# Splitting the second norm of a decoder layer: the first 128 tokens' norm, queries and scores ahead of the other columns

## Chip, cores and metric

The kernel runs on one core of a Trainium2 chip. The metric is device time in microseconds (us) of one launch; lower is better. The core has five engines with queues of their own: TensorE (PE, matmuls), VectorE (DVE), ScalarE (ACT), GpSimd (POOL, which here issues the gathers) and SyncE (SP, which issues the weight loads). They meet at semaphores, and 16 DMA engines move the data.

## Reference

One layer of a decoder over 288 tokens (256 of a prompt, 8 samples of 4), D = 1024: adaLN norm, one input projection, a short convolution and a sparse attention, merged and projected, then a second norm and a retrieval of single-neuron experts (PEER). The change touches the last part:

```python
def _peer(h, w_q, sub_keys, u_tab, v_tab):
    ...
    def block_fn(hb):
        q = (hb @ w_q).reshape(PEER_BLOCK, PEER_HEADS, 2, PEER_QDIM // 2).astype(jnp.float32)
        s = jnp.einsum('thpd,phkd->thpk', q, sub_keys.astype(jnp.float32))
        s1, i1 = lax.top_k(s[:, :, 0], PEER_TOPK)
        s2, i2 = lax.top_k(s[:, :, 1], PEER_TOPK)
        ...
        e = jnp.take_along_axis(cidx, top_pos, axis=-1)
        g = jax.nn.softmax(top_s, axis=-1)
        act = jax.nn.gelu(jnp.einsum('thkd,td->thk', u_tab[e], hb).astype(jnp.float32))
        return jnp.einsum('thk,thkd->td', (g * act).astype(hb.dtype), v_tab[e])
...
    h2 = _modulate(_rmsnorm(x, norm2_w), shift2, scale2)
    y = _peer(h2.reshape(-1, D_MODEL), peer_w_q, peer_sub_keys, peer_u, peer_v).reshape(x.shape)
```

Each token picks 8 heads x 16 experts, and for each expert one row of `peer_u` and one of `peer_v` (1024 floats, 4 KB) is read from memory.

## The kernel before

Everything is float32. Activations of the second half are kept transposed: `xT` and `hT` are 8 blocks of 128 channels by columns of tokens (columns 0 to 255 the prompt, 256 to 287 the samples; `hT` has 96 more columns, copies of the samples, so that the third group of tokens fills 128 rows too).

**The second norm.** PE makes the output projection block by block (L800), DVE adds it to `xT` and writes `hT` = `xT` times the scale (L1591 to L1598), ACT squares (L1208), PE sums the squares with a matrix of ones (L499), ACT takes the root of all 288 columns (`deviation`, L1069, into `rstd`). DVE then inverts `rstd` (L1317), multiplies the samples' columns and shifts them (L1602, L1603), and goes through the 8 channel blocks of `hT` with the 256 prompt columns: times `rstd` (L1605), plus the shift (L1607), one signal of `h_ready` each. L1608 makes the copies of the samples.

**Queries and scores.** PE computes 16 query blocks, `j` = 0 to 15, of 8 matmuls with 288 columns each (L843; the trace shows each float32 matmul as two rows). ACT copies each into `qpT` (L1241). `turn_h2(0)` (L832) turns the first 128 tokens of `hT` into rows for the dot products. `score_unit(n)` (L825) multiplies the queries of unit n with the sub-keys; units 0 and 1 are heads 0 and 1 of the first 128 tokens, from unit 2 on a unit has two heads. ACT copies the scores (L1221) and DVE does `route(n)`: top 16 of both sides, top 16 of their sums, and the experts' numbers into `eidx` (L1617 to L1682), at whose end `routed` goes up by one. `SCORE_AFTER` says after which `j` a unit's scores come.

**The gathers.** A slot is one expert of each of 128 tokens. There are 288 slots, 16 to a head, and each needs an indirect DMA of 128 rows of `peer_u` (L1012, `ask_u`) and one of `peer_v` (L1023, `ask_v`), 512 KB each, issued by POOL in one fixed order: u alone at first, v for slot j from u slot j + 12 or so on, then by turns. In this text u16 is the u gather of slot 16, v8 the v gather of slot 8, and so on. `urows` is a ring of NU = 10 buffers, `vrows` one of NV = 13. u gather i waits for the dot product of slot i - 10 (`u_used`); the first of a unit also waits for `routed` (u0, u16, u32, ...). v4 to v7 lie where the weights of queries `j` = 8 to 11 are, and v8 to v11 where those of `j` = 12 to 15 are, so v4 and v8 wait until PE is done with them. DVE's `dot(i)` (L1726) waits for u gather i and multiplies it with the turned tokens; ACT does the gelu and makes diagonal matrices (L1273), and PE adds up the v rows (L894, L896) once all 16 query blocks are done.

**DVE's order.** After the norm: `route(0)`, `route(1)`, then `dot(0)`, `dot(1)`, ... with steps of the next `route` in between: a `route` is a generator with 16 steps, of which two follow each dot while the unit's first slot is within 26.

## Time and profile before

| what | value |
|---|---|
| median of three runs | 1178.35 us (1177.5 to 1179.29) |
| the profiled execution | 1175.52 us, of which its span is 1173.7 us |
| PE busy | 987.4 us (84%) |
| DVE busy | 718.2 us (61%) |
| POOL busy | 573.8 us (49%) |
| ACT busy | 243.1 us (21%) |
| mean DMA rate over the span | 324 GB/s |
| moved by the queue of indirect DMAs | 312.92 MB of 379.90 MB |

The busy shares are means over stages that have different limits, so none of them alone says what sets the time. The 40 slices of the profile's page, 29.3 us each, show the stages; the chain of waits shows who waits for whom in one of them. Times inside the trace are counted from the start of the span.

### The profile page before, as it was taken

The numbers are of one execution on the slowest core, as the hardware profiler recorded it, in microseconds if no ns is written. First come the engines' busy times: TensorE is split into PE (matmuls) and PEld (weight loads), VectorE is DVE, ScalarE is ACT, GpSimd is POOL, SyncE is SP. The second block draws the span as 40 slices with busy tenths as digits, with TensorE's granted clock in tenths as the row PEclk, the third lists the DMA queues.
The fourth block names the chain that finished last, engine by engine and source line by source line (L and its number), as shares of the span: only waits on it lengthen the run. The fifth ranks groups of instructions, "written<-read, shape, count | busy, mean of one in ns | idle before, by whom it ended". The sixth has DMA issues, their size and how long they took to land.

```text
span 1173.7 us, 10777 instructions
## 1 busy us (share of the span) xinstructions
PE 987.4 (84%) x3369; PEld 497.0 (42%) x3369; DVE 718.2 (61%) x1750; ACT 243.1 (21%) x588; POOL 573.8 (49%) x618
## 2 busy tenths in 40 slices
PE   6898888998999999998787777777777777778888
PEld 3346766675677675452232222222222222223233
DVE  3248465888453699757657658568467576544442
ACT  2111222214401123333112111112112121121110
POOL 0201001002000166777777777777777777777750
PEclk9899999999999999999999999999999999999999
DMA  9952333778354499999999999999999999999993
GB/s 334 332 179 79 111 111 126 251 239 278 93 180 170 160 396 339 409 409 409 409 409 409 409 409 410 408 410 410 409 409 408 410 409 409 410 409 409 409 409 157
DMA packets 121324, 379.90 MB, mean 324 GB/s; under 512 B 11580, under 2 KB 21048, under 8 KB 121268
## 3 DMA queue, kind: packets, MB, share of 16 engines
q0 software_dynamic: 86208, 312.92, 68.0%
q1 hardware_dynamic: 34886, 66.19, 16.2%
q8 instruction: 28, 0.46, 0.2%
q14 instruction: 28, 0.23, 0.1%
q10 hardware_dynamic: 174, 0.11, 0.0%
HBM read 377.59 MB, written 1.59 MB: 323 GB/s over the span
## 4 chain that ended last, share of the span: by engine, by line
DMA 34%; PE 34%; POOL 13%; DVE 10%; issue 6%; ACT 2%; SPq 0%; DVEq 0%; ACTq 0%; POOLq 0%
DMA big<-peer_v,oT 16%; DMA big<-peer_u,oT 14%; PE twoA L556 7%; POOL big L1023 7%; POOL big L1012 5%; PE twoD L894 4%; PE twoD L896 4%; PE twoD L800 3%; DMA big<-w_ada 2%; DVE big L1726 2%; PE twoA L534 2%; PE twoA L843 2%; PE twoA L483 2%; PE twoA L704 1%; DMA r<-peer_u,oT 1%
## 5 line engine op out<-in xcount | busy, mean ns | idle before, releaser
L1012 POOL DMA_INDIRECT big<-peer_u,oT x232 | 220.0, 948 | 196.5 <-DVEq L1684 116.6
L1023 POOL DMA_INDIRECT big<-peer_v,oT x266 | 250.4, 941 | 87.9 <-issue 67.4
L1726 DVE CUSTOM_DVE_ANT_0 big<-big,twoA 128x1024 f32<-128x1024 f32 x128 | 156.3, 1221 | 138.8 <-DMA big<-peer_u,oT 137.8
L1726 DVE CUSTOM_DVE_ANT_0 big<-big,twoD 128x1024 f32<-128x1024 f32 x104 | 125.5, 1218 | 58.2 <-DMA big<-peer_u,oT 57.2
L894 PE MATMUL twoD<-big 128*128 128x512 f32 x176 | 97.7, 637 | 44.2 <-DMA big<-peer_v,oT 42.4
L556 PE MATMUL twoA<-hT,big 128*128 128x288 f32 x448 | 116.5, 417 | 0.0
L894 PE MATMUL twoD<-big,modT 128*128 128x512 f32 x132 | 73.2, 637 | 31.1 <-DMA big<-peer_v,oT 30.8
L556 PEld LDWEIGHTS twoA<-hT,big 128*128 128x128 f32 x448 | 85.5, 195 | 28.4 <-issue 5.9
L896 PE MATMUL twoD<-big 128*128 128x512 f32 x176 | 89.9, 592 | 0.0
L894 PEld LDWEIGHTS twoD<-big 128*128 128x128 f32 x176 | 27.0, 188 | 110.4 <-DMA big<-peer_v,oT 105.1
L896 PE MATMUL twoD<-big,modT 128*128 128x512 f32 x132 | 67.4, 592 | 0.0
L894 PE MATMUL twoD<-big,rstd 128*128 128x512 f32 x90 | 49.8, 635 | 19.8 <-DMA big<-peer_v,oT 19.4
L894 PE MATMUL twoD<-big,cT 128*128 128x512 f32 x88 | 48.2, 630 | 21.4 <-DMA big<-peer_v,oT 20.8
L1273 ACT ACTIVATE big<-ctab,oT 128x128 f32<-128x128 f32 x96 | 34.1, 393 | 137.5 <-DVE oT L1705 89.9
L1012 POOL DMA_INDIRECT r<-peer_u,oT x56 | 53.4, 954 | 18.4 <-issue 12.5
L1726 DVE CUSTOM_DVE_ANT_0 r<-r,twoA 128x1024 f32<-128x1024 f32 x32 | 39.0, 1220 | 36.6 <-DMA r<-peer_u,oT 36.6
L1273 ACT ACTIVATE modT<-ctab,oT 128x128 f32<-128x128 f32 x72 | 26.3, 394 | 137.0 <-DVE oT L1705 92.6
L894 PEld LDWEIGHTS twoD<-big,modT 128*128 128x128 f32 x132 | 20.1, 188 | 80.2 <-DMA big<-peer_v,oT 75.8
L896 PEld LDWEIGHTS twoD<-big 128*128 128x128 f32 x176 | 33.4, 190 | 42.1 <-issue 42.1
L843 PE MATMUL twoA<-hT,big 128*128 128x288 f32 x192 | 49.0, 410 | 1.8 <-DVE hT L1607 1.8
L896 PE MATMUL twoD<-big,rstd 128*128 128x512 f32 x90 | 46.0, 592 | 0.0
L896 PE MATMUL twoD<-big,cT 128*128 128x512 f32 x88 | 44.9, 592 | 0.0
(339 smaller groups left out, 1415.6 us busy)
## 6 DMA issues: line engine op xcount, KB each, us to landing
big<-w_ada SPq DMA_DIRECT2D x8, 2048.0 KB, 8.0
big<-w_in SPq DMA_DIRECT2D x5, 2048.0 KB, 8.9
big<-w_in SPq DMA_DIRECT2D x9, 1024.0 KB, 7.5
big<-w_ada SPq DMA_DIRECT2D x2, 4096.0 KB, 23.4
big<-peer_w_q SPq DMA_DIRECT2D x3, 2048.0 KB, 8.4
big<-peer_v,oT POOLq DMA_INDIRECT x266, 19.7
big<-w_out SPq DMA_DIRECT2D x2, 2048.0 KB, 11.5
big<-peer_u,oT POOLq DMA_INDIRECT x232, 17.6
```

The costliest lines, as they stand in the source:

```text
L483: mm = pe.matmul(b[32 * q:32 * q + 32, :], cT[:, k, :], w[:, k, :], start=(k < 4), stop=(k >= 4), skip_group_check=True)
L534: mm = pe.matmul(b[:, 0:width], hT[:, k, COLS[t]:COLS[t] + P], w[:, k, :], start=(k == 0), stop=(k == DC - 1))
L556: mm = pe.matmul(b[:, 0:TOK], w[:, k, j * P:(j + 1) * P], hT[:, k, 0:TOK], start=(k == 0), stop=(k == DC - 1))
L704: mm = pe.matmul(b[:, 0:TOK], slot[0][:, k, j * P:(j + 1) * P], aT[:, k, 0:TOK], start=(k == 0), stop=(k == 3))
L800: mm = pe.matmul(b[:, 0:TOK], w[:, k, (j % 4) * P:(j % 4 + 1) * P], mixT[:, k, :], start=(k == 0), stop=(k == DC - 1))
L843: mm = pe.matmul(b[:, 0:TOK], w[:, k, (j % 4) * P:(j % 4 + 1) * P], hT[:, k, 0:TOK], start=(k == 0), stop=(k == DC - 1))
L894: pe.matmul(acc[0][:, :], diag[j % NDG], row[:, 0:512], start=(s == 0), stop=(s == SLOTS[t] - 1), skip_group_check=True)
L896: mm = pe.matmul(acc[1][:, :], diag[j % NDG], row[:, 512:D], start=(s == 0), stop=(s == SLOTS[t] - 1), skip_group_check=True)
L1012: pool.indirect_dma_start(urows[i % NU], None, peer_u, bass.IndirectOffsetOnAxis(ap=eidx[:, t, s:s + 1], axis=0)).then_inc(u_in[i % NU], 16)
L1023: pool.indirect_dma_start(vrows[j % NV], None, peer_v, bass.IndirectOffsetOnAxis(ap=eidx[:, t, s:s + 1], axis=0)).then_inc(v_in[j % NV], 16)
L1273: act.activation(diag[j % NDG], ident, ACT.Copy, scale=dots[:, t, s:s + 1]).then_inc(diag_ready, 1)
L1726: dve.tensor_tensor_reduce(out=urows[i % NU], in0=urows[i % NU], in1=h2tok[t][:, :], scale=1.0, scalar=0.0, op0=ALU.mult, op1=ALU.add, acc ...
```

## The change

Four things change. (1) The norm after the root is done for columns 0 to 127 first: DVE inverts 128 columns of `rstd`, then goes through the 8 channel blocks with the product of block c ahead of the shift of block c - 1. The other columns follow: inversion of 160, 8 products of 160 columns (`h_scaled`), and ACT, no longer DVE, adds the shift to columns 128 to 255 (`shift_rest`, `h_rest`). (2) PE makes query blocks 0 and 1 for the 128 columns, turns the first tokens, and scores unit 0; only then it makes the 160 other columns of blocks 0 and 1 and goes on with `j` = 2. Turning the sub-keys is spread around the sum of squares, and one of the four turns still waits for the root. (3) DVE does `route(0)`, the copies of the samples, and then dots at once; `route(1)` is cut in: no step after dots 0 to 3, three steps after each dot from 4 on. (4) The u ring begins with buffers that no query weights use, so that u0 no longer waits for the first query weights to be free; u6 does.

```diff
+        urows = urows[4:] + urows[:4]
...
-        H2_BEFORE = 2
+        SUB_ORDER = (0, 2, 1, 3)
...
-        SCORE_AFTER = [1, 4, 8, 12]
+        SCORE_AFTER = [4, 8, 12]
...
             square_sum(DC - 2, 1)
+            pe.wait_ge(sub_landed, 16)
+            turn_sub(SUB_ORDER[0])
+            square_sum(DC - 1, 1)
+            turn_sub(SUB_ORDER[1])
+            turn_sub(SUB_ORDER[2])
+            pe.wait_ge(sd_ready, 2)
+            turn_sub(SUB_ORDER[3])
...
+            first = weights(pe, group("peerq"))
+            for j in range(2):
+                b = A.open(pe)
+                for k in range(DC):
+                    pe.wait_ge(h_ready, DC + k + 1)
+                    mm = pe.matmul(b[:, 0:P], first[:, k, j * P:(j + 1) * P], hT[:, k, 0:P], start=(k == 0), stop=(k == DC - 1))
+                A.close(mm)
+            pe.wait_ge(d_free, V.n)
+            turn_h2(0)
+            score_unit(0)
+            pe.wait_ge(h_ready, 2 * DC + 1)
             for j in range(16):
...
+                b, begin = A.open(pe), P if j < 2 else 0
                 for k in range(DC):
                     if j == 0:
-                        pe.wait_ge(h_ready, DC + k + 1)
+                        pe.wait_ge(h_rest, k + 1)
...
@@ gathers, POOL @@
+                if i == 6:
+                    pool.wait_ge(*released[group("peerq")])
...
-            pool.wait_ge(*released[group("peerq")])
+            pool.wait_ge(*released[group("out", 1)])
...
@@ ScalarE @@
+            for j in range(2):
+                copy_query(j, 0, P)
+            for c in range(4):
+                shift_rest(c)
+            copy_scores()
+            for c in range(4, DC):
+                shift_rest(c)
             for j in range(16):
...
+                copy_query(j, P if j < 2 else 0, TOK)
...
@@ VectorE @@
-            inverse(2)
+            dve.wait_ge(sd_ready, 2)
+            L.tell(dve.reciprocal(rstd[:, 0:P], rstd[:, 0:P]))
+            for c in range(DC + 1):
+                if c < DC:
+                    L.tell(tt(hT[:, c, 0:P], hT[:, c, 0:P], rstd[:, 0:P], ALU.mult), wait=False)
+                if c:
+                    L.done_but(1 if c < DC else 0)
+                    L.tell(ts(hT[:, c - 1, 0:P], hT[:, c - 1, 0:P], modT[:, 23 + c, 0:1], None, ALU.add), h_ready, wait=False)
+            L.tell(dve.reciprocal(rstd[:, P:TOK], rstd[:, P:TOK]))
+            for c in range(DC):
+                L.tell(tt(hT[:, c, P:TOK], hT[:, c, P:TOK], rstd[:, P:TOK], ALU.mult), h_scaled, wait=False)
...
-            for n in range(2):
-                for _ in route(n):
-                    pass
-            found, router = 2, route(2)
+            for _ in route(0):
+                pass
+            L.tell(cp(hT[:, :, TOK:3 * P].rearrange("p c (r t) -> p c r t", t=NSM),
+                      hT[:, :, SEQ:TOK].unsqueeze(2).broadcast_to([P, DC, 3, NSM])), h_ready)
+            found, router = 1, route(1)
...
-                for _ in range(2 if near <= 26 else (1 if found > 2 and near < 44 else 0)):
+                for _ in range((0 if i < 4 else 3) if found == 1 else 2 if near <= 26 else (1 if found > 2 and near < 44 else 0)):
```

On PE, this is what stood between the turned sub-keys and query block 3 (the names after the operation are what it writes and what it reads; `x7` is the number of further matmuls of the block):

```order
L843 MATMUL twoA<-hT,big 128x288 [waits h_ready,a_free,w_landed5]
L843 MATMUL twoA<-hT,big 128x288 [waits h_ready] x7
L843 MATMUL twoA<-hT,big 128x288 [waits a_free]
L843 MATMUL twoA<-hT,big 128x288 x7
L832 MATMUL twoD<-ctab,hT 128x128 [waits h_ready,d_free]
L832 MATMUL twoD<-ctab,hT 128x128 x7
L825 MATMUL twoA<-zall,r 128x128 [waits a_free,qp_ready,subT_ready]
```

And the same place after the change:

```order
L810 MATMUL twoA<-ctab,zall 128x128 [waits a_free,sd_ready]
L810 MATMUL twoA<-ctab,zall 128x128 x3
L846 MATMUL twoA<-hT,big 128x128 [waits h_ready,a_free,w_landed5]
L846 MATMUL twoA<-hT,big 128x128 [waits h_ready] x7
L838 MATMUL twoD<-ctab,hT 128x128 [waits h_ready,d_free]
L838 MATMUL twoD<-ctab,hT 128x128 x7
L831 MATMUL twoA<-zall,r 128x128 [waits a_free,qp_ready,subT_ready]
L860 MATMUL twoA<-hT,big 128x160 [waits a_free,h_rest,w_landed5,h_ready]
L860 MATMUL twoA<-hT,big 128x160 [waits h_rest] x7
```

The scores of unit 0 (L831) now stand behind two blocks of 128 columns, and the blocks of 160 columns behind the scores.

On DVE, right behind the end of `route(0)` (L1681, L1682 before), the whole of `route(1)` stood ahead of the first dot:

```order
L1681 CAST oT<-zall 128x16 [waits dve_seq]
L1682 TENSOR_TENSOR zall<-zall,gsm 128x16
L1617 MAX zall<-r 128x8 [waits s_ready]
L1617 MAX zall<-r 128x8
L1621 MAX_INDEX zall<-zall,r 128x8 [waits dve_seq] x2
```

After the change the dots (two rows each, L1768; `u_in4` is the semaphore of a u buffer) stand there, and `route(1)` between them:

```order
L1724 TENSOR_TENSOR zall<-zall,gsm 128x16
L1773 COPY hT<-hT 128x8x96 [waits dve_seq]
L1768 ISA big,oT<-big,twoD 128x1024 [waits u_in0,h2_ready,h_ready]
...
L1768 ISA r,oT<-r,twoD 128x1024 [waits u_in4]
L1768 ISA oT 128x1
L1659 MAX zall<-r 128x8 [waits s_ready]
L1659 MAX zall<-r 128x8
L1663 MAX_INDEX zall<-zall,r 128x8 [waits dve_seq] x2
L1667 MATCH_REPLACE r<-zall,r 128x128 [waits dve_seq] x2
L1768 ISA r,oT<-r,twoD 128x1024 [waits u_in5]
```

The end of `route(1)`, which u16 waits for, moved from ahead of dot 0 to behind dot 9; the first step of `route(2)` follows it directly.

On POOL the first gathers were eight, two and six u gathers, v0 and u16:

```order
L1012 DMA big<-peer_u,oT 128x1024 [waits routed,a_full]
L1012 DMA big<-peer_u,oT 128x1024 x7
L1012 DMA r<-peer_u,oT 128x1024 x2
L1012 DMA big<-peer_u,oT 128x1024 [waits u_used] x6
L1023 DMA big<-peer_v,oT 128x1024
L1012 DMA big<-peer_u,oT 128x1024 [waits u_used,routed]
```

They are now

```order
L1029 DMA big<-peer_u,oT 128x1024 [waits routed,d_full]
L1029 DMA big<-peer_u,oT 128x1024 x3
L1029 DMA r<-peer_u,oT 128x1024 x2
L1029 DMA big<-peer_u,oT 128x1024 [waits a_full]
L1029 DMA big<-peer_u,oT 128x1024 x3
L1029 DMA big<-peer_u,oT 128x1024 [waits u_used] x4
L1029 DMA r<-peer_u,oT 128x1024 [waits u_used] x2
L1040 DMA big<-peer_v,oT 128x1024
L1029 DMA big<-peer_u,oT 128x1024 [waits u_used,routed]
```

The order of slots is the same; the wait for the query weights (`a_full`) moved from u0 to u6.

## Rows read from the trace of the kernel before

**Rows 1.** The page: DMA rate in 40 slices of 29.3 us.

```profile
GB/s 334 332 179 79 111 111 126 251 239 278 93 180 170 160 396 339 409 409 409 409 409 409 409 409 410 408 410 410 409 409 408 410 409 409 410 409 409 409 409 157
```

**Rows 2.** Stretches: length, then busy us of each engine, granted clock, DMA share, GB/s.

```profile
405.00:410.00 5.00, 5.00 (x24) 4.01 (x23) 2.56 (x18) 0.80 (x2) 3.78 (x5) 1.00 0.65 202
410.00:415.00 5.00, 5.00 (x23) 3.90 (x22) 4.79 (x19) 0.75 (x2) 3.78 (x5) 1.00 0.95 313
415.00:440.00 25.00, 25.00 (x113) 19.98 (x112) 24.48 (x84) 6.29 (x13) 17.00 (x18) 1.00 1.02 409
440.00:460.00 20.00, 17.89 (x68) 12.07 (x67) 19.71 (x54) 8.95 (x22) 12.51 (x15) 1.00 0.90 306
480.00:1150.00 670.00, 533.46 (x1180) 194.26 (x1179) 410.94 (x976) 127.59 (x337) 491.88 (x521) 1.00 1.03 409
```

**Rows 3.** POOL in order of time: u0, u1, u16, u24, v8.

```profile
404.73 0.94 POOL L1012 DMA_INDIRECT big<-peer_u,oT  x1 [116.64 <-DVEq L1684]
405.97 0.94 POOL L1012 DMA_INDIRECT big<-peer_u,oT  x1 [0.30 <-issue]
...
426.47 0.94 POOL L1012 DMA_INDIRECT big<-peer_u,oT  x1 [0.30 <-issue]
...
449.10 0.94 POOL L1012 DMA_INDIRECT big<-peer_u,oT  x1 [1.03 <-DVE oT L1726]
...
454.73 0.93 POOL L1023 DMA_INDIRECT big<-peer_v,oT  x1 [0.30 <-issue]
```

**Rows 4.** The tile peer_u, 400 to 470 us: from issue to landing.

```profile
DMA to landing us min/median/max: 4.1/6.6/7.9
```

**Rows 5.** DVE in order of time: the norm, both first routes, dots, route 2.

```profile
380.13 1.95 DVE L1317 RECIPROCAL rstd<-rstd 128x288 f32<-128x288 f32 x1 [1.37 <-ACT rstd L1069]
...
383.37 0.35 DVE L1607 TENSOR_SCALAR hT<-hT,modT 128x256 f32<-128x256 f32 x1
383.64 0.42 DVE L1605 TENSOR_TENSOR hT<-hT,rstd 128x256 f32<-128x256 f32 x1
...
395.31 0.49 DVE L1617 MAX8 zall<-r 128x8 f32<-128x128 f32 x2 [6.07 <-ACT r L1221]
...
407.40 0.49 DVE L1617 MAX8 zall<-r 128x8 f32<-128x128 f32 x2 [3.51 <-ACT r L1221]
...
415.83 0.17 DVE L1682 TENSOR_TENSOR zall<-zall,gsm 128x16 f32<-128x16 f32 x1
416.28 1.22 DVE L1726 CUSTOM_DVE_ANT_0 big<-big,twoD 128x1024 f32<-128x1024 f32 x1 [0.28 <-DVE zall L1682]
...
423.13 1.22 DVE L1726 CUSTOM_DVE_ANT_0 big<-big,twoD 128x1024 f32<-128x1024 f32 x1
...
446.99 0.18 DVE L1682 TENSOR_TENSOR zall<-zall,gsm 128x32 f32<-128x32 f32 x1
```

**Rows 6.** PE in order of time: query blocks, turn, scores.

```profile
383.87 9.59 PE L843 MATMUL twoA<-hT,big 128*128 128x288 f32 x32 [1.75 <-DVE hT L1607]
393.30 1.04 PE L832 MATMUL twoD<-ctab,hT 128*128 128x128 f32 x8
394.17 0.61 PE L825 MATMUL twoA<-zall,r 128*128 128x128 f32 x4
394.62 7.93 PE L843 MATMUL twoA<-hT,big 128*128 128x288 f32 x32
...
439.53 11.81 PE L843 MATMUL twoA<-hT,big 128*128 128x288 f32 x48
```

**Rows 7.** ACT in order of time: copies of query 1, of its scores, gelu 1.

```profile
393.50 0.41 ACT L1241 ACTIVATE r<-twoA 128x288 f32<-128x288 f32 x1 [3.47 <-PE twoA L843]
394.82 0.38 ACT L1221 ACTIVATE r<-twoA 128x256 f32<-128x256 f32 x1 [0.91 <-PE twoA L825]
...
450.53 0.21 ACT L1237 ACTIVATE oT<-oT 128x8 f32<-128x8 f32 x1 [7.29 <-DVE oT L1726]
```

**Rows 8.** A stretch near the start, columns as in group 2.

```profile
40.00:50.00 10.00, 7.34 (x27) 3.68 (x28) 7.21 (x22) 0.80 (x2) 0.77 (x1) 0.66 1.07 373
```

More of the change, by code:

```diff
@@ L804, in _, with turn_sub @@
                     square_sum(j - 2, 1)
-            square_sum(DC - 2, 1)
-            square_sum(DC - 1, 1)
-            pe.wait_ge(sd_ready, 2)
-            pe.wait_ge(sub_landed, 16)
-            for q in range(4):
+            def turn_sub(q):
                 b = A.open(pe)
@@ L838, in _ @@
                     w = weights(pe, g)
-                b = A.open(pe)
+                b, begin = A.open(pe), P if j < 2 else 0
                 for k in range(DC):
                     if j == 0:
-                        pe.wait_ge(h_ready, DC + k + 1)
-                    mm = pe.matmul(b[:, 0:TOK], w[:, k, (j % 4) * P:(j % 4 + 1) * P], hT[:, k, 0:TOK], start=(k == 0), stop=(k == DC - 1))
+                        pe.wait_ge(h_rest, k + 1)
+                    mm = pe.matmul(b[:, begin:TOK], w[:, k, (j % 4) * P:(j % 4 + 1) * P], hT[:, k, begin:TOK], start=(k == 0),
+                                   stop=(k == DC - 1))
                 A.close(mm)
                 released[g] = (a_full, A.n)
-                if j == H2_BEFORE - 1:
-                    pe.wait_ge(d_free, V.n)
-                    turn_h2(0)
                 if j in SCORE_AFTER:
-                    score_unit(SCORE_AFTER.index(j))
+                    score_unit(SCORE_AFTER.index(j) + 1)
             score_unit(4)
@@ L1208, in _, with copy_sub @@
                 L.tell(act.activation(sq[:, c * TOK:(c + 1) * TOK], xT[:, c, :], ACT.Square), sq_ready)
-            deviation(1)
-            act.wait_ge(sub_landed, 16)
-            for q in range(4):
+            def copy_sub(q):
                 b = A.take(act)
@@ L1215, in _ @@
                 act.sem_inc(a_free, 1)
+            act.wait_ge(sub_landed, 16)
+            copy_sub(SUB_ORDER[0])
+            deviation(1)
+            for q in SUB_ORDER[1:]:
+                copy_sub(q)
             def copy_scores():
@@ L1237, in gelus, with copy_query, shift_rest @@
                 L.tell(act.activation(chunk, chunk, ACT.Gelu_apprx_tanh), gelu_done, wait=False)
+            def copy_query(j, a, e):
+                b = A.take(act)
+                L.tell(act.activation(qpT[:, j, a:e], b[:, a:e], ACT.Copy), qp_ready)
+                act.sem_inc(a_free, 1)
+            def shift_rest(c):
+                act.wait_ge(h_scaled, c + 1)
+                L.tell(act.activation(hT[:, c, P:SEQ], hT[:, c, P:SEQ], ACT.Identity, bias=modT[:, 24 + c, 0:1]), h_rest, wait=False)
+            for j in range(2):
[5 more added lines that the diff above has]
+                shift_rest(c)
             for j in range(16):
-                b = A.take(act)
-                L.tell(act.activation(qpT[:, j, :], b[:, 0:TOK], ACT.Copy), qp_ready)
-                act.sem_inc(a_free, 1)
+                copy_query(j, P if j < 2 else 0, TOK)
                 if j in SCORE_AFTER:
@@ L1599, in _ @@
                           ab[:, j, 1:9].unsqueeze(2).broadcast_to([P, NB, NS]), ALU.mult), wait=False)
[L1600 to L1609 removed]
+            dve.wait_ge(sd_ready, 2)
[9 more added lines that the diff above has]
+                L.tell(tt(hT[:, c, P:TOK], hT[:, c, P:TOK], rstd[:, P:TOK], ALU.mult), h_scaled, wait=False)
+            dve.wait_ge(h_scaled, DC)
+            hs = hT[:, :, SEQ:TOK].rearrange("p c (b s) -> p c b s", s=NS)
+            L.tell(tt(hs, hs, modT[:, 24:24 + DC, 1:9].unsqueeze(3).broadcast_to([P, DC, NB, NS]), ALU.add), h_ready)
             def top16(n, values, best, place):
```

15 lines of the change are left out of this document (4 added, 11 removed).

## The prediction

> **What bounds the kernel now.** I read the slices of the page first: from the 17th on the DMA engines move 409 GB/s without a break almost to the end [rows 1]. From 480 to 1150 us the DMA share is 1.03 while PE, DVE and POOL all have idle time [rows 2]. So the long second part is a fixed quantity of bytes at a fixed rate: 576 gathers of 0.524 MB at 409 GB/s, 1.281 us each, 738 us in all. PE's tail behind the last gather stays as it is. What can change is when the gathers begin, and how much DMA time is lost until the queue is full for good.
>
> The stretches give both. u0 is issued at 404.73 [rows 3]. From there to 415 the engines move 2.58 MB in 10.3 us, which at full rate are 6.3: a cold start costs 4.0. Then 409 GB/s up to 440; from 440 to 460 it is 306, a loss of 5.0 [rows 2]. The sum over these stretches is 18.9 MB, 36 gathers, which in POOL's order are u0 to u26 and v0 to v8. **My yardstick: in the kernel before, gather 36 is through at 460.0, and from then on nothing is lost.** If it is through earlier by x in the changed kernel, and nothing is lost later, the kernel is faster by x.
>
> The loss from 440 to 460 is DVE's. POOL waits for a dot ahead of u24 [rows 3], because from 424.3 to 447.2 DVE has only seven dots (7 to 13) beside the 16 steps of `route(2)` [rows 5].
>
> **The change step by step.**
>
> *The start of the gathers.* Today the inversion of 288 columns begins at 380.13 and takes 1.95; a product of 256 columns takes 0.42 and a shift 0.35, with 0.27 between the starts of two that don't wait for each other [rows 5]. Of 128 columns the inversion is about 0.95 (in proportion, and a little fixed): 381.1. With products and shifts interleaved none waits for its predecessor, so a pair is between 0.27 (two instructions at 256 columns' 0.27, halved) and 0.45. I take 0.32: first product 0.3, eight pairs 2.6, last shift ready at 384.2. PE follows with query 0 (ends 384.4). The trace has matmuls of 128 columns in the scores and the turn: the turn's 8 rows take 0.87 from start to start of the next, 0.11 each [rows 6]. Query 1 is 16 such rows, 1.8: 386.2. The turn makes it 387.1, the scores 387.6 and 387.8 to their end. ACT has copied query 1 by 386.7, does four shifts of some 0.25 and is free at 387.8; copying the scores takes 0.38 [rows 7]. DVE begins `route(0)` at 388.4 instead of 395.31 [rows 5]: 6.9 earlier. Nothing between it and u0 changes except that u0 needs no query weights: u0 at 397.8.
>
> *The second route.* Today `route(1)` ends at 416.0 [rows 5], and u16 needs it only at 426.47 [rows 3], so it holds no gather up. Now dots 0 to 4 come first. A u gather takes 4.1 to 7.9 from issue to landing, median 6.6 [rows 4]; by bytes five gathers are through 10.4 after u0's issue [rows 2], and u4's issue at +5.0 with the median is +11.6. I take 11.2: dot 4 runs from 409.0 to 410.2. The 16 steps of `route(1)` have five dots (5 to 9) between them. The route takes 8.6 alone (407.40 to 416.0) and a dot 1.14 [rows 5], together 14.3: `routed` at 424.5, and u16 0.8 later, as u0 after `route(0)`, at **425.3**. POOL, issuing every 1.24 [rows 3], has u0 to u15 and v0 out by 418.9; the engines are through with these 17 at 397.8 + 4.0 + 21.8 = 423.6 and run dry. So the early start turns into a wait, and u16 comes only 1.2 earlier than today.
>
> *After it.* 19 gathers remain to number 36. A second cold start of 4.0 and 19 x 1.281 = 24.3 give 453.6, if POOL isn't held up. DVE then holds nothing up: at 424.5 it has done 10 dots and two routes, today 7 at 424.3. `route(2)` with seven dots takes 22.9 as today, so dot 16 is done at about 445, and u26 wants it at 425.3 + 17 x 1.24 = 446.4. The loss of 5.0 goes.
>
> *PE's queries.* v8 would be issued at 447.6, but its buffer holds query weights until block 15 is done. The 160-column blocks can start behind the scores and the samples' shift at about 387.9; 32 rows of 0.135 (0.243 for 288 columns, in proportion [rows 6]) take 4.3, so block 2 starts at 392.3 instead of 394.6, if ACT's last four shifts (388.2 to 389.2) keep ahead, as they do by a hair. Everything behind is as before, hence block 15 ends at 449.0 instead of 451.3 [rows 6], and v8 goes out at 449.3. Today v8 is issued at 454.73 [rows 3] and is through 5.3 later. The same 5.3 gives **454.6**, later than 453.6. The later one decides: x = 5.4.
>
> *Edits at nothing.* The first turn of sub-keys and its copy lie in PE's wait for the last square; if that cover fails, up to 0.7 on the start. The copies for the samples (0.55) lie between `route(0)` and the landing of u0, the shifts moved to ACT in its idle time ahead of the scores. u6 waits for block 3, which ends at about 400.1 against u6 at 405.2. ACT's gelu 1 waits for dot 15 (today until 450.53 [rows 7]), now at about 441, so PE's banks are freed sooner.
>
> **Rule against trace.** In the trace a shift starts 0.27 after the one ahead when it needn't wait for it [rows 5]: a fixed part is hidden. The Trainium skill, "VectorE: DVE Perf Modes", section on the TRN2 errata, says the reverse of such splits: each instruction on SBUF pays a fixed latency between instructions, so that small tiles pay it more often, and for a float32 product it gives (N + 151) / 0.96 ns. This case's row agrees for 256 columns alone (0.42). As an estimate by that page, a pair of 128 columns would be 0.58 and the start 2.1 later; u16 at 427.4, the 36th gather at 455.7, x = 4.3. By the rows it is 5.4, which I keep. The difference is small because v8's wait swallows it.
>
> **Unknown costs and their bounds.** The pair on DVE: 0.27 to 0.45, the start -0.4 to +1.0. The second cold start: 4.0 when it is as the first; not below 2.9 (4.1 to the first landing less one transfer). Shifts on ACT: if PE waits for each, block 2 is up to 1.5 later, x down to 3.9. Stalls for dots, today 5.0: from none to all. A pause of POOL at v8 on top of a queue filled only since 425: nothing to 1.2. Good ends together give x = 7.1 (v8 at its 447.6), bad ones without the stalls 2.8.
>
> **The rivals.**
> - *A, forecast:* u16 waits for the later `route(1)`, the stalls at 440 to 460 go, v8 waits for PE. 1175.5 - 5.4 = 1170.1 in the profiled execution's own time, 1173.0 as a median (the shown one lies 2.8 above the profiled time). Chance 0.50, own range 1171.2 to 1175.0.
> - *B, more is kept:* `route(1)` ends sooner than I think (landings quicker, steps hidden behind dots), the queue doesn't run dry, and PE finishes some us earlier too. For it speaks the start lead of 6.9, against it block 15, tied to 57 us of PE's work from block 2 on. x = 7 to 9, 1170.3. Chance 0.15.
> - *C, the gain drains away:* DVE is again late with dots behind u16, since the same work lies ahead of slot 32. Part or all of the 5.0 comes back: x = 0.4 to 2.4, 1177.0. For it speaks that DVE has only 1.4 to spare at u26; against it that the DMA backlog covers a pause of POOL. Chance 0.20. Here belongs also that the start comes hardly earlier: u16 is tied to u0 at +27.5, and with u0 after 401 no 2.4 is left.
> - *D, slower:* TensorE's clock. It is granted in full (1.00, the 2.4 GHz level) in this stretch although PE waits for DVE there [rows 2]. From 40 to 50 us, where PE was busy 7.34 of 10 with short groups and gaps, the grant was 0.66, a part of it at the 1.2 GHz level [rows 8]. The new 378 to 389 has such short groups. At the lower level PE loses half its time: 11 us of it shift v8 to 454.8, and the gain is gone; with 16 us v8 goes out at 457.3 and the kernel is 2.6 slower, 1181.0. Chance 0.07.
> - The rest, 0.08, is spread over both sides.
>
> **The numbers.** A measurement of this kernel tells some 0.2% (2.4 us) from no change. Faster by more: A, B, and a little of C and the rest, 0.77; within: most of C, 0.16; slower: D and a bit, 0.07. The range for 8 in 10 goes from B's low end to the middle of C: 1169.5 to 1177.2.
>
> **What would show it.** u0 at 397.8 (wrong beyond 1.0), `route(0)` from 388.4. POOL waiting some 6 us ahead of u16, for DVE, until 425.3; a hole in the DMA rate at about 424 to 429. No wait for a dot at u20 to u26. v8 released by PE at about 449.3, block 2 starting at 392.3. From 460 on 409 GB/s as today, and the last gather 5.4 earlier. It is wrong if u16 comes after 430, if the rate from 440 to 460 is again near 306, or if the granted clock falls below 1.00 between 380 and 450.

## The result, and the profile of the changed kernel

The changed kernel takes 1170.3 us as the median of 8 runs (1169.63 to 1175.08), the kernel before 1177.41 beside it (8 runs, 1176.27 to 1180.62): a ratio of 0.9942, 95% interval 0.9927 to 0.9957, 6.8 us faster (5.1 to 8.6). The two medians stand 7.1 apart. The forecast was 5.4 us and 1173.0. The profiled execution took 1169.63 us, its span 1167.8: 5.9 less than that of before.

The page, DMA rate in 40 slices. The rate is steady from the 17th slice on, as in [rows 1], and at the same height; the three slices ahead of it moved more than before (238, 346 and 380 GB/s against 160, 396 and 339).

```profile
GB/s 332 339 177 79 128 94 127 252 234 283 97 181 148 238 346 380 410 409 409 409 409 410 408 410 409 409 410 410 409 409 409 410 409 409 409 409 410 408 410 162
```

Stretches, columns as in [rows 2]: length, busy us of each engine, granted clock, DMA share, GB/s.

```profile
398.00:405.00 7.00, 7.00 (x33) 5.58 (x32) 1.80 (x3) 1.06 (x3) 5.48 (x6) 1.00 0.72 225
405.00:410.00 5.00, 5.00 (x22) 3.95 (x21) 4.23 (x7) 0.55 (x2) 3.78 (x5) 1.00 0.99 355
410.00:420.00 10.00, 10.00 (x43) 7.79 (x43) 9.79 (x39) 0.82 (x2) 6.61 (x8) 1.00 1.02 411
420.00:435.00 15.00, 15.00 (x68) 11.96 (x67) 14.62 (x61) 5.23 (x9) 8.09 (x9) 1.00 0.81 284
435.00:450.00 15.00, 14.50 (x66) 11.31 (x65) 14.70 (x41) 5.12 (x9) 10.39 (x11) 1.00 1.03 410
450.00:460.00 10.00, 8.70 (x22) 4.08 (x22) 10.00 (x36) 4.62 (x14) 7.56 (x9) 0.83 0.94 324
460.00:480.00 20.00, 20.00 (x46) 7.79 (x45) 13.05 (x41) 5.48 (x12) 15.12 (x17) 1.00 1.03 410
480.00:1150.00 670.00, 536.86 (x1189) 196.38 (x1188) 413.99 (x983) 128.41 (x340) 487.67 (x517) 1.00 1.02 408
```

The forecast hole is there: 284 GB/s from 420 to 435. The stalls of 440 to 460 are gone up to 450 (410 GB/s); from 450 to 460 a smaller hole is left, 324.

POOL in order of time: u0, v0, u16, v7, the u gather behind it, v8; in brackets the idle time ahead and what ended it.

```profile
397.91 0.94 POOL L1029 DMA_INDIRECT big<-peer_u,oT  x1 [110.75 <-DVEq L1726]
...
417.80 0.94 POOL L1040 DMA_INDIRECT big<-peer_v,oT  x1 [0.30 <-issue]
424.47 0.93 POOL L1029 DMA_INDIRECT big<-peer_u,oT  x1 [5.73 <-DVEq L1726]
...
444.88 1.40 POOL L1040 DMA_INDIRECT big<-peer_v,oT  x1 [0.30 <-issue]
446.58 0.94 POOL L1029 DMA_INDIRECT big<-peer_u,oT  x1 [0.31 <-issue]
449.38 0.94 POOL L1040 DMA_INDIRECT big<-peer_v,oT  x1 [1.86 <-PE twoA L860]
```

POOL waits 5.73 us at u16 for the end of `route(1)` (the signal behind L1724, which is L1726), as the forecast said, then for no dot, and 1.86 at v8 for PE's last query block.

DVE in order of time: the norm of 128 columns, that of 160, the first steps of `route(0)`, dots 0 and 4, the end of `route(1)`, and the first step of `route(2)`.

```profile
379.80 0.95 DVE L1639 RECIPROCAL rstd<-rstd 128x128 f32<-128x128 f32 x1 [1.33 <-ACT rstd L1086]
...
382.58 0.28 DVE L1642 TENSOR_TENSOR hT<-hT,rstd 128x128 f32<-128x128 f32 x1
382.79 0.28 DVE L1645 TENSOR_SCALAR hT<-hT,modT 128x128 f32<-128x128 f32 x1
382.98 0.28 DVE L1642 TENSOR_TENSOR hT<-hT,rstd 128x128 f32<-128x128 f32 x1
...
385.15 1.97 DVE L1648 TENSOR_TENSOR hT<-hT,rstd 128x160 f32<-128x160 f32 x8
...
388.50 0.49 DVE L1659 MAX8 zall<-r 128x8 f32<-128x128 f32 x2 [0.92 <-ACT r L1243]
...
402.16 1.22 DVE L1768 CUSTOM_DVE_ANT_0 big<-big,twoD 128x1024 f32<-128x1024 f32 x1 [4.37 <-DMA big<-peer_u,oT]
...
408.89 1.22 DVE L1768 CUSTOM_DVE_ANT_0 r<-r,twoD 128x1024 f32<-128x1024 f32 x1
...
423.97 0.17 DVE L1724 TENSOR_TENSOR zall<-zall,gsm 128x16 f32<-128x16 f32 x1
424.29 0.87 DVE L1659 MAX8 zall<-r 128x8 f32<-128x128 f32 x4
```

PE in order of time: the short blocks, turn, scores of unit 0, then the 160 other columns of blocks 0 and 1 together with blocks 2 and 3 (one row of 64), and the last three blocks.

```profile
381.62 4.79 PE L846 MATMUL twoA<-hT,big 128*128 128x128 f32 x32 [1.10 <-DVE hT L1645]
386.25 1.04 PE L838 MATMUL twoD<-ctab,hT 128*128 128x128 f32 x8
387.12 0.61 PE L831 MATMUL twoA<-zall,r 128*128 128x128 f32 x4
387.63 12.68 PE L860 MATMUL twoA<-hT,big 128*128 128x160 f32 x64
...
437.30 11.81 PE L860 MATMUL twoA<-hT,big 128*128 128x288 f32 x48
```

**A closer yardstick.** The part of the program ahead of the norm is the same in all kernels but for the turning of the sub-keys, but its length differs between profiled executions: DVE's inversion of `rstd` (I call its start the root) begins at 379.6 to 383.1 us. So I count from the root: u0; then the DMA time lost between u0 and 480, which is that stretch less its bytes at 409 GB/s; then the end of the span. For the changed kernel the rows above hold 29.3 MB, 71.7 us at 409 GB/s, and 480 - 397.9 - 71.7 = 10.4. For the kernel before, [rows 2] give 9.0 up to 460. The other rows of the table are worked out in the same way. The granted clock over the span is 0.984 to 0.988 in them; the last column is explained below the table.

| kernel | u0 | lost | sum | end | end less sum | ratio to before | faster than before, all executions at clock 0.987 |
|---|---|---|---|---|---|---|---|
| before | 24.6 | 9.0 | 33.6 | 793.6 | 760.0 | | |
| changed | 18.1 | 10.4 | 28.5 | 788.0 | 759.5 | 0.9942 | 5.3 (with e5) |
| changed, e5 | 18.1 | 9.9 | 28.0 | 787.0 | 759.0 | 0.9945 | |
| e6, five steps | 18.1 | 15.7 | 33.9 | 794.0 | 760.1 | 0.9994 | 0.6 |
| e7, five steps, v ring | 18.1 | 15.4 | 33.5 | 793.2 | 759.7 | 0.9994 | 0.7 |
| e8, old u ring | 20.8 | 8.7 | 29.5 | 788.8 | 759.3 | 0.9952 | 3.9 |
| e9, steps mended | 18.1 | 10.1 | 28.2 | 788.1 | 759.9 | 0.9953 | 5.7 |
| e10, mended, v ring | 18.1 | 7.7 | 25.8 | 785.5 | 759.7 | 0.9932 | 8.0 |
| e11, v ring | 18.1 | 8.9 | 27.0 | 786.2 | 759.2 | 0.9937 | 6.7 |
| e12, `route(1)` first | 18.1 | 13.5 | 31.6 | 791.5 | 759.9 | 0.9978 | 2.8 |

What is left behind the sum is 759.0 to 760.1 us in all ten. So the end is set by when the gathers begin and by the DMA time lost until the queue stays full, and by nothing else that these edits touch. The sum is an account and no forecast: it takes the lost time from the same trace as the end. From before to changed the start gains 6.5 and the losses take 1.4 back, which leaves 5.1; 5.6 arrive at the end of the span, and the 0.5 between them is within the 1.1 by which the rest differs from profile to profile. The ratio says 6.8, with both inside its interval.

**A second measure, from all executions.** The account rests on one profile of each kernel. The times of all executions bear it out once the granted clock is taken out. Within each kernel a lower mean clock over the span goes with a longer time: 0.97 us for each 0.001 (0.90 to 1.04), by a straight line of one slope through 132 executions (the changed kernel's eight of the result and all of the second and third rounds below). The profiles show where that time lies: the root is at 382.5 to 383.1 us in the four executions at 0.984 and 0.985 (e6, e8, e10, e11) and at 379.6 to 381.7 in the six at 0.987 and 0.988, while "end less sum" is alike in both groups. So it lies ahead of the root. The last column of the table compares all executions at one clock, 0.987, with intervals of 0.5 to 0.7 to both sides; "at one clock" means this comparison from here on. The kernel before stands at 1177.0 us at that clock in the second round and at 1176.9 in the third, so kernels of the two rounds can be compared in this way. The column agrees with the differences of "sum" within 0.9 us in every row, and it tells kernels apart that the ratios alone don't.

### The profile page after: what moved, and what is told of

The parts are those of the page before. It is cut to its first block, busy times and chain, and to the rows that moved or that the text cites. A ratio compares the mean times of both kernels' runs of the same rounds, so it can differ in the third digit from the quotient of the medians.

```text
span 1167.8 us, 10869 instructions
## 1 busy us (share of the span) xinstructions
PE 987.6 (85%) x3401; PEld 500.4 (43%) x3401; DVE 717.3 (61%) x1758; ACT 246.0 (21%) x598; POOL 574.3 (49%) x618
## 4 chain that ended last, share of the span: by engine, by line
PE 39%; DMA 37%; POOL 11%; DVE 6%; issue 5%; ACT 2%; SPq 0%; DVEq 0%; ACTq 0%; POOLq 0%
DMA big<-peer_v,oT 20%; DMA big<-peer_u,oT 12%; PE twoA L557 7%; POOL big L1040 5%; PE twoA L860 5%; PE twoD L909 5%; PE twoD L911 5%; POOL big L1029 4%; PE twoD L801 3%; DMA big<-w_ada 2%; PE twoA L535 2%; PE twoA L484 2%; PE twoA L705 1%; PE twoD L789 1%; POOL r L1029 1%
## 5 line engine op out<-in xcount | busy, mean ns | idle before, releaser
L1029 POOL DMA_INDIRECT big<-peer_u,oT x230 | 217.3, 945 | 188.9 <-DVEq L1726 116.5
L1768 DVE CUSTOM_DVE_ANT_0 big<-big,twoA 128x1024 f32<-128x1024 f32 x128 | 156.3, 1221 | 142.0 <-DMA big<-peer_u,oT 141.0
L1768 DVE CUSTOM_DVE_ANT_0 big<-big,twoD 128x1024 f32<-128x1024 f32 x102 | 123.2, 1217 | 51.3 <-DMA big<-peer_u,oT 50.0
L557 PE MATMUL twoA<-hT,big 128*128 128x288 f32 x448 | 116.0, 415 | 0.0
L909 PEld LDWEIGHTS twoD<-big 128*128 128x128 f32 x176 | 27.5, 190 | 108.2 <-DMA big<-peer_v,oT 101.2
L1768 DVE CUSTOM_DVE_ANT_0 r<-r,twoA 128x1024 f32<-128x1024 f32 x32 | 39.1, 1221 | 33.3 <-DMA r<-peer_u,oT 33.3
L860 PE MATMUL twoA<-hT,big 128*128 128x288 f32 (+1 forms) x192 | 44.2, 390 | 0.0
```

Of the source, the lines that this page charges most:

```text
L557: mm = pe.matmul(b[:, 0:TOK], w[:, k, j * P:(j + 1) * P], hT[:, k, 0:TOK], start=(k == 0), stop=(k == DC - 1))
L860: mm = pe.matmul(b[:, begin:TOK], w[:, k, (j % 4) * P:(j % 4 + 1) * P], hT[:, k, begin:TOK], start=(k == 0), stop=(k == DC - 1))
L909: pe.matmul(acc[0][:, :], diag[j % NDG], row[:, 0:512], start=(s == 0), stop=(s == SLOTS[t] - 1), skip_group_check=True)
L1029: pool.indirect_dma_start(urows[i % NU], None, peer_u, bass.IndirectOffsetOnAxis(ap=eidx[:, t, s:s + 1], axis=0)).then_inc(u_in[i % NU], 16)
L1768: dve.tensor_tensor_reduce(out=urows[i % NU], in0=urows[i % NU], in1=h2tok[t][:, :], scale=1.0, scalar=0.0, op0=ALU.mult, op1=ALU.add, acc ...
```

## The experiments

Twelve runs in three rounds; each run is a set of executions with one of them profiled. In the first round (e1 to e4) the chip granted PE a mean clock of 0.904 to 0.911 over the span, the steady rate was 368 GB/s instead of 409, and the kernel before took 1261.64 us. Its runs are compared with each other alone. In the second the kernel before took 1178.56 us, in the third 1177.76.

**e1, the changed kernel again.** No edit.

> The changed kernel once more, as the yardstick for the kernels of this group. By the accounts of gathers (36 of them through 5.4 us earlier) it should be 5.4 to 7 us faster than the kernel before, ratio 0.994 to 0.9955.

1253.44 us, ratio 0.9938 (0.9918 to 0.9958). The gain is there, but the trace isn't that of the first run: u16 is 49.5 behind the root instead of 44.7, though u0 is at 18.1 in both. Two stretches of e1:

```profile
420.00:425.00 5.00, 1.44 (x6) 0.84 (x5) 1.86 (x5) 0.41 (x1) 2.81 (x4) 1.00 1.03 412
425.00:430.00 5.00, 3.60 (x8) 2.47 (x8) 4.03 (x13) 0.82 (x2) 0.00 (x0) 0.66 0.71 283
```

PE is busy 1.44 of 5 us and DVE 1.86 while the DMA engines are full; PE's rows name no semaphore there but "issue", up to 2.38 us at a time. ACT stands still first: it copies a query block every 3.9 us, at 409.23 for the last time, and begins the next copy only at 421.92, while PE runs on until 421. This lengthens `route(1)`. What the three engines waited for isn't shown.

**e2, `route(1)` ahead of the dots**, in the changed kernel.

```diff
+            for _ in route(1):
+                pass
-            found, router = 1, route(1)
+            found, router = 2, route(2)
...
-                for _ in range((0 if i < 4 else 3) if found == 1 else 2 if near <= 26 else (1 if found > 2 and near < 44 else 0)):
+                for _ in range(2 if near <= 26 else (1 if found > 2 and near < 44 else 0)):
```

> The changed kernel with the second route again ahead of the first dot. Theory (the lead is kept because DVE does ten dots before the route of unit 2, which takes the stalls at u20 to u26 away): u0 stays at 397.9; the route starts with its scores at 405 and ends at 413.8, dot 0 at 415, u10 waits for it, u16 goes out at 423.9, half a us earlier than in the changed kernel; but then everything is the kernel before shifted by 2.5 us, with POOL waiting for dots ahead of u18 to u25, v8 at 452.3: 2.5 us faster than before, 3 us slower than the changed kernel. Rival (only the early start counts, the place of the second route is neutral): as fast as the changed kernel, 5 to 7 us faster than before.

1254.23 us, 0.993 (0.9902 to 0.9957): not to be told from e1. The waits for dots were back in its trace, but e1 had the stall just shown, and this round couldn't weigh one against the other.

**e3, the new order alone**: parts 3 and 4 of the change on the kernel before, the norm unsplit.

```diff
+        urows = urows[4:] + urows[:4]
...
+                if i == 6:
+                    pool.wait_ge(*released[group("peerq")])
...
-            pool.wait_ge(*released[group("peerq")])
+            pool.wait_ge(*released[group("out", 1)])
...
-            for n in range(2):
-                for _ in route(n):
-                    pass
-            found, router = 2, route(2)
+            for _ in route(0):
+                pass
+            found, router = 1, route(1)
...
-                for _ in range(2 if near <= 26 else (1 if found > 2 and near < 44 else 0)):
+                for _ in range((0 if i < 4 else 3) if found == 1 else 2 if near <= 26 else (1 if found > 2 and near < 44 else 0)):
```

> The kernel before with the other two parts alone: the second route between the dots and the u ring turned round, but the norm, queries and scores as before. Theory (u16 hangs on u0 by 26.6 us): u0 at 404.7, u16 at 431.3, a hole in the DMA rate of 6 us of POOL's time ahead of it, no stall for dots later, v8 at about 454: no change, -0.3 to +0.2%. Rival (the new order of DVE is worth the 5 us of stalls by itself): 3 to 5 us faster than before.

1264.89 us, 1.0028 (1.0014 to 1.0043): a little slower. The rival is out; the upper end of my theory's range, 0.2% slower, lies inside the interval, but u16 went out at 441.44 and not at 431.3. Its profile has the stall of e1 in a worse form, and behind it a hole. Here PE's row names ACT, whose copy of a block that was done at 423.9 begins at 434.16:

```profile
430.00:435.00 5.00, 0.38 (x2) 0.38 (x2) 2.20 (x7) 0.72 (x2) 0.93 (x1) 0.57 1.03 410
435.00:440.00 5.00, 5.00 (x21) 4.19 (x21) 4.90 (x16) 3.23 (x5) 0.00 (x0) 0.75 0.14 52
...
434.62 2.08 PE L826 MATMUL twoA<-zall,r 128*128 128x128 f32 x8 [6.88 <-ACT r L1244]
```

The order alone wasn't run again in a later round, so whether it is slower at the higher clock stays open. It is shown only that in this round it brought nothing by itself.

**e4, v ring**: the one v buffer on which no query weights lie moved from the 13th place of the ring to the 5th, so that v8 lies where blocks 8 to 11 were, and v9 is the first to wait for block 15.

```diff
-        vrows += [part(D)]
+        vrows.insert(4, part(D))
+        v_wring.insert(4, v_wring.pop())
```

> The changed kernel with the v buffer that does not lie in the last query weights moved from place 12 to place 4 of the ring, so that v9 and not v8 is the first to wait for query block 15. Theory (the pause of 1.9 us ahead of v8 costs the 2.1 us that the DMA engines lose between 450 and 460): POOL does not wait at v8 nor at v9 (due at 450.3, block 15 ends at 449.1), the rate is 409 GB/s from 435 on, 1.5 to 2 us faster than the changed kernel. Rival (the queue is deep enough, the loss at 450 to 460 has another cause): no change against the changed kernel.

1252.94 us, 0.9928 (0.9904 to 0.9952), against 0.9938 of e1: not told apart.

**e5, the changed kernel a third time**, with e6 to e8.

> The changed kernel again as the yardstick of this group: ratio 0.993 to 0.9955 to the kernel before.

1171.94 us against 1178.56, 0.9945 (0.9925 to 0.9966). u0 and v8 stand at the same distance from the root as in the first run, within 0.01, and u16 0.34 later.

**e6, `route(1)` faster**: five steps after each dot from dot 2 on.

```diff
-                for _ in range((0 if i < 4 else 3) if found == 1 else 2 if near <= 26 else (1 if found > 2 and near < 44 else 0)):
+                for _ in range((0 if i < 2 else 5) if found == 1 else 2 if near <= 26 else (1 if found > 2 and near < 44 else 0)):
```

> The changed kernel with five steps of the second route after each dot from dot 2 on, in place of three from dot 4 on. The route then ends behind dot 5: u16 at 421.0 instead of 424.5. Theory (v8 is released by query block 15 at 449.1 whatever POOL does before it, and decides): POOL waits 6 us at v8 instead of 1.9, the DMA engines run dry there, no change against the changed kernel, within 0.5 us. Rival (the hole ahead of u16 decides): 3.4 us faster than the changed kernel.

1178.11 us, 0.9994 (0.997 to 1.0018): the whole gain gone, and both expectations missed. DVE of e6, the end of `route(1)` and what stands behind it:

```profile
422.34 0.21 DVE L1724 TENSOR_TENSOR zall<-zall,gsm 128x16 f32<-128x16 f32 x1
424.44 0.87 DVE L1659 MAX8 zall<-r 128x8 f32<-128x128 f32 x4 [1.89 <-ACT r L1243]
...
427.31 1.21 DVE L1768 CUSTOM_DVE_ANT_0 big<-big,twoD 128x1024 f32<-128x1024 f32 x1
```

And its POOL: u15, v0, u16, u17.

```profile
422.35 0.94 POOL L1029 DMA_INDIRECT r<-peer_u,oT  x1 [3.27 <-DVE oT L1768]
423.59 0.94 POOL L1040 DMA_INDIRECT big<-peer_v,oT  x1 [0.30 <-issue]
429.29 0.94 POOL L1029 DMA_INDIRECT big<-peer_u,oT  x1 [4.77 <-DVE oT L1768]
431.89 1.25 POOL L1029 DMA_INDIRECT big<-peer_u,oT  x1 [1.65 <-DVE oT L1768]
```

The last step of `route(1)` came 4.4 earlier (39.8 behind the root instead of 44.2), but the round of five ran on into `route(2)`, whose scores PE hadn't made: DVE stood 1.89 for them with dot 6 behind it, and u16 wants dot 6. From then on DVE was behind, u19 to u22 waited for dots too, and 15.7 us were lost instead of 10.4. This is rival C of the prediction in its worst form: the start is as early as ever, and all of it drains away.

**e7, e6 with the v ring.**

> Both: the free v buffer at place 4 of the ring and five steps from dot 2 on. v9 is now the first to wait for block 15, and goes out at 449.4 as gather 38 instead of v8 as gather 36. Theory: two gathers of 1.28 more are through by then, 2.0 to 2.6 us faster than the changed kernel. Rival (the hole ahead of u16 decides alone): 3.4 to 5 us faster than the changed kernel.

1176.71 us, 0.9994 (0.997 to 1.0017), and both expectations missed: u16 goes out 46.8 behind the root as in e6, for the reason of e6.

**e8, the old u ring**: u0 waits for the first query weights again.

```diff
-        urows = urows[4:] + urows[:4]
...
-                if i == 6:
-                    pool.wait_ge(*released[group("peerq")])
...
-            pool.wait_ge(*released[group("out", 1)])
+            pool.wait_ge(*released[group("peerq")])
```

> The changed kernel with the u ring in its old order, so that u0 waits for query block 3 (ends at 400.1): u0 at 400.4, 2.5 us later. Theory (u16 hangs on u0, but v8 hangs on block 15): u16 2.5 us later at 427.0, v8 unmoved at 449.4 and without its pause; 0.7 to 1.5 us slower than the changed kernel. Rival (the start counts in full): 2.5 us slower than the changed kernel.

1173.5 us, 0.9952 (0.9934 to 0.997); e5 beside it 1171.94. POOL of e8, u0:

```profile
403.48 0.93 POOL L1026 DMA_INDIRECT big<-peer_u,oT  x1 [112.86 <-PE twoA L859]
```

u0 is 2.7 later, the losses 1.2 to 1.7 smaller (v8 comes at 71.0 behind the root, block 15 has been done since 69.3, and POOL doesn't wait for it), and 0.8 to 1.8 are left at the end. The intervals of the ratios overlap, but at one clock e8 is 1.5 us slower than the changed kernel (0.8 to 2.1), as expected.

**e9, steps mended**: five steps, but the round stops where `route(1)` ends, and `route(2)` isn't begun before dot 10.

```diff
-                for _ in range((0 if i < 4 else 3) if found == 1 else 2 if near <= 26 else (1 if found > 2 and near < 44 else 0)):
+                for _ in range((0 if i < 2 else 5) if found == 1 else 0 if i < 10 else 2 if near <= 26 else (1 if found > 2 and near < 44 else 0)):
...
+                        if found == 2:
+                            break
```

> Edit: in the changed kernel no step of route(1) after dots 0 and 1, five after each dot from 2 on, and none of route(2) before dot 10 (in the five-step kernel the rest of the five went into route(2), which then held DVE for the scores of unit 2). Theory (the hole in the DMA rate is the end of route(1) with too many dots ahead of it; the five-step kernel failed only because route(2) was begun too early): route(1)'s 8.6 us begin at about 407 and have four dots in them, so routed at about 420 and u16, which also wants dot 6, at about 421 (changed kernel 424.5 to 426.7). The hole of 219 to 296 GB/s between 420 and 430 becomes small. From dot 10 on DVE is as in the changed kernel, so u26 waits some 2 us for dot 16, and v8 still goes out at 449 to 451, since PE's query blocks are as before. Hence no change against the changed kernel within 0.1% (ratio to the kernel before 0.994 to 0.995). Rival 1 (each us of u16 is kept): 3 us faster than changed, ratio 0.9915. Rival 2 (the order of dots is worth nothing but the slack, as in the five-step kernel): ratio 0.999.

1171.36 us, 0.9953 (0.9931 to 0.9974). POOL of e9, u15, v0, u16; then the u gather ahead of v8, and v8:

```profile
418.94 0.94 POOL L1029 DMA_INDIRECT r<-peer_u,oT  x1 [2.39 <-DVE oT L1768]
420.18 0.93 POOL L1040 DMA_INDIRECT big<-peer_v,oT  x1 [0.30 <-issue]
421.42 0.94 POOL L1029 DMA_INDIRECT big<-peer_u,oT  x1 [0.30 <-issue]
...
443.43 1.09 POOL L1029 DMA_INDIRECT big<-peer_u,oT  x1 [0.31 <-issue]
449.67 0.94 POOL L1040 DMA_INDIRECT big<-peer_v,oT  x1 [5.15 <-PE twoA L860]
```

And its stretches 420 to 435 and 450 to 460:

```profile
420.00:435.00 15.00, 15.00 (x67) 11.91 (x66) 14.83 (x55) 5.23 (x9) 10.58 (x12) 1.00 0.99 369
...
450.00:460.00 10.00, 8.70 (x22) 4.22 (x23) 10.00 (x36) 4.61 (x14) 7.56 (x9) 0.83 0.83 280
```

u16 comes 3.4 earlier (41.3 behind the root instead of 44.7), at the 421 expected, and the first hole nearly closes (369 instead of 284 GB/s). All of it stands again at v8, which waits 5.15 for PE instead of 1.86 and goes out at the same 69.6 behind the root. The end doesn't move: at one clock e9 is 0.4 us faster than the changed kernel, with an interval from 1.1 faster to 0.3 slower. (The 2 us that I expected u26 to wait for dot 16 didn't come: DVE, with its dots done sooner, was far enough ahead.) It also bears out why e6 fell: with `route(2)` kept back, the five steps cost nothing.

**e10, e9 with the v ring.** The edits of e9 and e4 together.

> Edit: the steps as in e9_steps_stop, and the v buffer that no query weights use moved from the 13th place of the ring to the 5th, so that v8 lies where blocks 8 to 11 were and v9 is the first that waits for block 15. Theory (v8's wait for PE decides the end once u16 isn't late): POOL isn't held at v8; v9 waits until 449, one or two gathers of the queue later, which the backlog of a queue that never ran dry covers. The lead at 460 grows from 5.4 to about 7.5 us: 1.5 to 3 us faster than the changed kernel, ratio to before 0.9915 to 0.993. Rival (PE or the dots are the bound by then, the earlier gathers only queue up): as the changed kernel, 0.994 to 0.995.

1168.82 us, 0.9932 (0.9907 to 0.9956), the lowest median of all. POOL of e10, v8 and v9:

```profile
448.56 0.93 POOL L1041 DMA_INDIRECT big<-peer_v,oT  x1 [0.30 <-PE twoA L861]
450.06 0.94 POOL L1030 DMA_INDIRECT big<-peer_u,oT  x1 [0.56 <-DVE oT L1769]
452.69 0.94 POOL L1041 DMA_INDIRECT big<-peer_v,oT  x1 [1.70 <-PE twoA L861]
```

v8 goes out 65.5 behind the root instead of 69.6. 7.7 us are lost instead of 9.9 to 10.4, and the end is 1.5 to 2.5 earlier than in the two profiles of the changed kernel: the size that the theory gave. By the ratios alone it isn't told apart from the changed kernel; at one clock it is 2.7 us faster (1.9 to 3.4). Its four executions at 0.987 and 0.988 took 1167.1 to 1168.8 us, the thirteen of the changed kernel 1169.6 to 1173.0. One part of the theory missed: the queue doesn't cover the 1.70 us that v9 waits, and the rate from 450 to 460 is 356 GB/s.

**e11, the v ring alone, again.**

> Edit: the changed kernel with the v buffer that no query weights use at the 5th place of the ring alone. Theory (v8's wait for PE decides the end, and the hole at u16 comes to nearly the same time, 453.6 by my sum against 454.6): 0.5 to 1.5 us faster than the changed kernel, ratio to before 0.993 to 0.994. Rival (the hole at u16 alone sets the end and v8's wait costs nothing): no change, 0.9945.

1170.37 us, 0.9937 (0.9914 to 0.996). 8.9 lost, the end 0.8 to 1.8 earlier by the profiles, again nothing that the ratio could tell; at one clock it is 1.4 us faster than the changed kernel (0.7 to 2.2). Its stretch from 450 to 460:

```profile
450.00:460.00 10.00, 8.20 (x25) 4.50 (x24) 9.74 (x31) 5.03 (x15) 7.48 (x9) 0.83 1.02 408
```

The clock is granted at 0.83 here as in the changed kernel, and the rate is whole. So the changed kernel's 324 GB/s there is v8's wait, not the clock; e5, the same kernel, has 370 GB/s there at a clock of 1.00, with 1.51 us of wait at v8 instead of 1.86.

**e12, `route(1)` ahead of the dots, again.** The edit of e2.

> Edit: in the changed kernel route(1) whole ahead of dot 0, two steps of route(2) after each dot, as in the kernel before. In the first round, where the clock was granted at 0.90, it was as fast as the changed kernel although the waits for dots had come back in its trace. Theory (the stalls of 440 to 460 cost what the trace shows, 5.0 us less what the later u16 of the changed kernel gives up): u16 at 420 to 422, no hole before it, rate 440 to 460 about 300 GB/s, 3 us slower than the changed kernel, ratio to before 0.9965 to 0.998. Rival (the order of route(1) and dots is worth nothing, the hole only moves): as the changed kernel, 0.994 to 0.995.

1173.99 us, 0.9978 (0.9962 to 0.9994): slower than the changed kernel by 0.33 to 0.36% as the ratios stand, some 4 us, and by 2.6 at one clock (1.9 to 3.2); 3 were expected. The stretches of e12:

```profile
410.00:420.00 10.00, 10.00 (x44) 7.85 (x43) 9.59 (x28) 0.83 (x3) 3.76 (x5) 1.00 0.74 269
420.00:435.00 15.00, 15.00 (x68) 11.90 (x67) 14.93 (x58) 5.11 (x9) 10.52 (x12) 1.00 0.97 374
435.00:450.00 15.00, 14.13 (x64) 11.00 (x63) 14.61 (x40) 5.12 (x9) 7.71 (x10) 1.00 0.92 323
```

The hole lies ahead, 269 GB/s from 410 to 420, where POOL waits 5.33 us for dot 0 at u10, and from 435 to 450 the waits for dots are back (323 instead of 410). My expectation had no hole ahead and u16 at 420 to 422. The hole costs 3.4 us of DMA time, and u16 goes out at 424.10, no earlier than in the changed kernel. PE's query blocks run as in the changed kernel, all 0.2 us earlier as the root is. PE's work is the same and the DMA's losses differ, so the end is the gathers', though the chain of waits of the changed kernel goes through PE's query blocks for 63% of the time from 376 to 470.

## Why the prediction was right

**The start: right, with two sizes off by little.** u0 stands at 397.91 against 397.8, `route(0)` at 388.50 against 388.4. Two small things cancel in it: this execution reached the root 0.33 earlier than that of before, and the pair on DVE takes 0.40, not 0.32. (The prediction's own terms, 381.1, 0.3 and 2.6, make 384.0 and not 384.2 for the last shift; it was ready at 384.05.) The rows show why: product and shift last 0.28 each and start 0.20 apart. From the root the lead is 6.5, not 6.9. The Trainium skill, "VectorE: DVE Perf Modes", section on the TRN2 errata, puts the fixed latency between instructions. Its formula, which the page gives for a float32 add, agrees here with the length of one product, (128 + 151) / 0.96 = 0.29. The 0.58 that I had worked out from it for a pair doesn't come about: the trace has 0.40, between that and my value.

**`route(1)` and u16: right.** Dot 4 starts at 408.89 (409.0), u16 at 424.47 (425.3); POOL waits 5.73 us ("some 6"). The last signal of `route(1)` comes at 424.1 (424.5), and u16 0.3 behind it and not 0.8. The hole is there and a little smaller than forecast: the sum had 1.7 us of empty queue ahead of u16 and 4.0 behind, 5.7 in all; from 420 to 435 284 GB/s instead of 409 are 4.6, of which 3.7 lie behind u16's issue. e9 shows that the wait is the end of `route(1)`: with it earlier, u16 follows.

**The stalls for dots: right.** No gather waits for a dot between u16 and v8. e12 prices this step of the change at 2.6 us at one clock, 3.5 to 4.5 by the profiles, some 4 by the ratios. Without it the split of the norm and the u ring bring 0.22% alone, 2.8 us at one clock.

**PE's queries and v8: the order right, and the step on which all hangs.** The short blocks end at 386.4, scores and turn at 387.7, block 15 at 449.1 (449.0), v8 goes out at 449.38 (449.3), released by PE. "The later one decides" is what e9 to e11 show: u16 3.4 earlier alone brings nothing, v8's buffer free alone 1.4 at one clock, both together 2.7. The chance for B, that more would be kept, rested on PE finishing earlier; it didn't.

**The loss at v8: two misses that cancel.** The sum took the 5.3 us from v8's issue to gather 36 being through over from the kernel before, where the queue was full: 449.3 and 5.3 are 454.6. By the bytes, the 36 gathers were through at 452.9 in the changed kernel, 3.5 behind v8's issue and near the other term, 453.6. But the yardstick's second half, "from then on nothing is lost", didn't hold: POOL's pause at v8, kept at "nothing to 1.2", makes a rate of 324 GB/s from 450 to 460, a loss of 2.1, of which 1.6 fall behind gather 36. 452.9 and 1.6 are 454.5 (5.5 earlier than 460.0, or 5.1 from the root, which this execution reached 0.33 earlier). So the wait that decides was rightly named, but that x comes out as 5.1 by the closer yardstick, 5.6 by the end of the span and 5.3 by all executions at one clock, for a forecast of 5.4, is in part luck.

**C and D.** C didn't come, but e6 shows how near it lay: 1.89 us of DVE at the wrong place bring it, with 5.3 more lost and 0.9994 as the ratio. DVE's little room was the right thing to worry about, though the place was u16 and not u26. One sentence under C was wrong: with u0 after 401 there was to be no 2.4 left. The prediction's own sum, 401 + 27.5 + 4.0 + 24.3 = 456.8, leaves 3.2, and e8, whose u0 stands at 400.9 on the clock of the kernel before (20.8 behind the root), is 3.9 faster than before at one clock. D: the grant was 1.00 through the short groups of 380 to 390, as it was there in the kernel before ([rows 2], which the prediction names for it, begin only at 405). It fell behind block 15, where PE stands still from 449.1 to 452.1 but for the last scores, and there it cost the gathers nothing (e11); in e5, the same kernel, it didn't fall.

**The total.** The median lies 2.7 below the 1173.0: 0.9 of it is that the kernel before itself ran at 1177.41 here and not at 1178.35, the rest is between the 5.4 of the forecast and the 7.1 of the medians. At one clock the changed kernel is 5.3 us faster (4.8 to 5.8), so the forecast's gain is met, and the rest is most likely the mix of granted clocks in the two sets. That isn't shown for this very comparison, since the granted clock is not known for the eight executions of the kernel before.

## What to carry to other kernels

In a kernel whose second half is a queue that never may run dry, write down two numbers: when the queue begins, and how much of its time is lost until it stays full. Here they gave the end of ten executions to within 1.1 us, while the chain of waits went mostly through PE's query blocks, which ran alike in the changed kernel and in e12, 3.5 us apart. When one wait is shortened, look for the next thing that holds the same queue before counting the gain: u16 earlier alone brought nothing, because v8 stood behind it. Count from an event just ahead of the change and look at each execution's granted clock before calling two kernels the same: most of the scatter here lay ahead of the root. And a generator that is advanced by a fixed number of steps runs across the end of its unit; what it then waits for stands ahead of work that was ready (e6).
